# Stick-breaking encoder layer: value matmuls one slot behind their transposes instead of two

## The chip, the cores and the metric

The kernel runs on one core of a Trainium2 chip. The metric is the device time of one execution in microseconds (us). Before the change its median over three runs is 1382.68 us (1381.59 to 1383.48).

The core has five engines that run side by side, each in its own program order, and wait for each other only through semaphores: TensorE (PE in the profile; its weight loads are listed apart as PEld), VectorE (DVE), ScalarE (ACT), GpSimd (POOL) and SyncE (SP), which issues DMAs. TensorE writes to PSUM, which here is eight banks of 128 x 512 float32.

## What is computed

One layer on 1024 tokens of 1024 features, float32: `x += norm(attention(norm(x)))`, then `x += norm(swiglu(norm(x)))`. The attention has 16 heads of 64. Its core, per head, with queries in rows:

```python
z = q @ k.T * scale
before = s < t                        # strictly causal
log_stay = where(before, log_sigmoid(-z), 0)
log_pass = reverse_cumsum(log_stay) - log_stay
a = where(before, exp(log_sigmoid(z) + log_pass), 0)
out = a @ v
```

## The kernel before

Tokens come in reversed order, so that the reverse cumulative sum is a forward scan. Heads are worked on in eight pairs. A pair has four groups: head 0 and 1 with the query rows X = (0, 1, 6, 7) in blocks of 128, then both with Y = (2, 3, 4, 5). Each group has five chunks of its 2304 score columns, so a pair has 20 **slots** and the stage 160, and a short tail of `TAIL_SLOTS` more finishes what is under way. The order of work in a slot is written out by hand, as a software pipeline over all engines. In slot s:

- PE, in this order: the value matmuls (AV, lines 1155 and 1157) of an earlier chunk; one part of the next pair's projections (three matmuls of 512 columns, lines 1083 to 1085); the transposes of a chunk of attention weights into a bank of TB (line 1181), in slots 6 and 9 also those of a piece of V (line 1168); the scores of slot s (lines 1200, 1201); the rest of the projection parts. `PARTS_UPTO` spreads 12 parts over five slots.
- ACT: copies the transposed chunk to `AT_hi`, rounded (line 464), computes two sigmoids of the scores (lines 568, 570), and has in some slots a copy of projected keys or queries, a value copy (line 524) or a weight split (line 456).
- DVE: subtracts `AT_hi` from the transposed chunk into `AT_lo` (line 837, both halves are multiplied with V), then the scans (line 924) and products (line 928) of whole query rows, in some slots the low halves of keys and queries (line 876) and a value addition (line 895).
- POOL: the low half of a split weight unit (line 734, 3 in a pair).

`T_LAG = 7`: the chunk transposed in slot s is the one whose scores were made seven slots before. `AV_LAG = 2`: its AV stand at the head of slot s + 2. There PE waits with `pe.wait_ge(t_lo, ...)` until its `AT_lo` is written. `AT_hi` and `AT_lo` have two buffers, by the parity of the slot. After a group's last AV, ACT copies half of the result (`O_COPY`) and DVE adds the other half (`O_ADD`), at slots fixed in two tables; the pair is counted beside the group, with -1 for the pair before. In the last pair no projections for a further pair are left, only V parts in its first slots. In the tail, PE does the first output projections (`WO_TAIL`, lines 1129 to 1131) between the last AV; they need `o_lo_t` (line 900), which needs `o_hi_t` (line 532) and the additions. The feed-forward part comes behind.

Of the kernel before, what the change touches and what calls it, by code (L numbers as in the profile page):

```python
# [101 lines left out]
def t_blocks(x, c):  # L102

    k, js = T_CHUNKS[x][c]
    out, at = [], 0
    for j in js:
        ks = [m for m in (k, k + 1) if ROWS[x][m] <= j]
        out.append((j, ks, at))
        at += P * len(ks)
    return out, at  # L110
# [17 lines left out]


T_LAG = 7  # L130
AV_LAG = 2
T_PER_STEP = SLOTS + 2
T_START = 2 * NT
V_SLOT = {6: 0, 9: 1}
# [2 lines left out]
def t_slot(s):  # L137

    at = (s - T_LAG) % SLOTS
    n = s + sum(v < s for v in V_SLOT)  # L140
    if s not in V_SLOT:
        return [(n, "a", at)]
    if V_SLOT[s] == 0:
        return [(n, "a", at), (n + 1, "v", 0)]
    return [(n, "v", 1), (n + 1, "a", at)]


def t_index(p, n):

    return T_START - T_LAG + T_PER_STEP * p + n  # L150
# [56 lines left out]

O_COPY = {14: (0, 0), 19: (0, 1), 4: (-1, 2), 9: (-1, 3)}  # L210
O_ADD = {15: (0, 0), 0: (-1, 1), 5: (-1, 2), 10: (-1, 3)}
TAIL_SLOTS = 11
TAIL_O = {0: 0, 1: 1}

WO_TAIL = {1: [(0, 0), (0, 1)], 2: [(0, 2), (1, 0)], 3: [(1, 1), (1, 2)],
# [34 lines left out]
def encoder_layer(nc, x, g_mix_pre, g_mix_post, g_ffn_pre, g_ffn_post, units, out):  # L250
    ctx = ExitStack()
    with ctx:
# [3 lines left out]
        def alloc(stack, name, shape, dt=F32):  # L256
            return stack.enter_context(nc.sbuf_tensor(name, shape, dt))
# [17 lines left out]
        with ExitStack() as one:  # L275
            A = alloc(one, "A", [P, 2, GROUP_W])
            with ExitStack() as qk:
# [10 lines left out]
                AT_hi = alloc(qk, "AT_hi", [P, 2, HALF], F32R)  # L288
                AT_lo = alloc(qk, "AT_lo", [P, 2, HALF], F32R)
# [162 lines left out]
        def _(act):  # L452
# [67 lines left out]
            def o_move(p, group):  # L520

                act.wait_ge(av_done, SLOTS * p + GROUP * (group + 1))
                o_p = acc[:, p, :] if isinstance(p, int) else acc[:, bass.ds(p, 1), :].rearrange("q a n -> q (a n)")
                nc.scalar.activation(values(o_p, group), values_bank(group, OTHER[GROUPS[group][0]]),
                                     ACT.Copy).then_inc(o_moved, 1)
# [8 lines left out]
            def step(p, par, first=False, proj=True, slots=SLOTS):  # L534
                tail = slots < SLOTS
                for s in range(slots):
# [42 lines left out]

                    if s in O_COPY and not (first and O_COPY[s][0] < 0):  # L580
                        dp, group = O_COPY[s]
                        o_move(p + dp, group)
# [15 lines left out]
            def split_at(m, waits):  # L598

                for s, v in waits:  # L600
                    act.wait_ge(s, v)
                split_hi(UNITS1 + m, ring(m), m % 2, 16 * ((UNITS1 + m) // 2 + 1))
# [3 lines left out]
            for t in range(2):  # L606
                act.dma_start(x_in[:, t, :], x_tiles[:, t, :]).then_inc(x_again[t], 16)
            step(PAIRS, 0, proj=False, slots=TAIL_SLOTS)
            split_at(0, [])
# [224 lines left out]
        def _(dve):  # L834
# [46 lines left out]
            def projections(p, par, s, first, proj):  # L881

                if s == 0 and not first:
                    qk_lo(4 * p + 4, "q", par, 1, ACCB[1])
                if proj and s in K_SLOT:
                    qk_lo(4 * p + 4 + K_SLOT[s] + 1, "k", 1 - par, K_SLOT[s], ACCB[K_SLOT[s]])
                if proj and s == Q_SLOT:
                    qk_lo(4 * p + 4 + 3, "q", 1 - par, 0, ACCB[0])

            def o_add(p, group):  # L890

                dve.wait_ge(o_moved, 4 * p + group + 1)
                o_p = acc[:, p, :] if isinstance(p, int) else acc[:, bass.ds(p, 1), :].rearrange("q a n -> q (a n)")
                o = values(o_p, group)
                nc.vector.tensor_tensor(o, values_bank(group, OWN[GROUPS[group][0]]), o, ALU.add).then_inc(o_done, 1)
# [7 lines left out]
            def step(p, par, first=False, proj=True, slots=SLOTS):  # L903
                tail = slots < SLOTS
                for s in range(slots):
# [23 lines left out]
                    if not tail:  # L929
                        projections(p, par, s, first, proj)  # L930
                    if s in O_ADD and not (first and O_ADD[s][0] < 0):
                        dp, group = O_ADD[s]
                        o_add(p + dp, group)
# [7 lines left out]
            step(PAIRS - 1, 1, proj=False)  # L941
            step(PAIRS, 0, proj=False, slots=TAIL_SLOTS)

# [111 lines left out]
        def _(pe):  # L1055
# [79 lines left out]
            def step(p, par, first=False, proj=True, slots=SLOTS):  # L1135
                tail = slots < SLOTS
                for s in range(slots):

                    dp, at = (0, s - AV_LAG) if s >= AV_LAG else (-1, s - AV_LAG + SLOTS)
                    if not (first and s < T_LAG + AV_LAG) and not (tail and s >= T_LAG + AV_LAG):  # L1140
                        z = (at - T_LAG) % SLOTS
                        h, x = GROUPS[z // GROUP]
                        g = next(n for n, kind, _ in t_slot(at) if kind == "a")
                        group = 4 * (p - (s < T_LAG + AV_LAG)) + z // GROUP
                        if z % GROUP == 0 and not (isinstance(group, int) and group < 2):

                            pe.wait_ge(o_done, group - 1)
                        pe.wait_ge(t_lo, t_index(p + dp, g) + 1)
                        blocks_, _ = t_blocks(x, z % GROUP)
                        for m, (j, ks, c0) in enumerate(blocks_):  # L1150
                            w = P * len(ks)
                            dst = OB[h][:, P * ks[0]:P * ks[0] + w]
                            v = V[:, j, 2 * h:2 * h + 2, :].rearrange("p a c -> p (a c)")
                            hi, lo = AT_hi[:, (s - T_LAG) % 2, c0:c0 + w], AT_lo[:, (s - T_LAG) % 2, c0:c0 + w]
                            nc.tensor.matmul(dst, v, hi, start=(z % GROUP == 0 and m == 0), stop=False,  # L1155
                                             skip_group_check=True)
                            mm = nc.tensor.matmul(dst, v, lo, start=False, stop=(z % GROUP == GROUP - 1 and m == 1),  # L1157
                                                  skip_group_check=True)
                        mm.then_inc(av_done, 1)
# [44 lines left out]
                    elif s in WO_TAIL:  # L1204
# [3 lines left out]
                        for t, j in WO_TAIL[s]:  # L1208
                            pe.wait_ge(w_ready, WO_UNIT + j + 1)
                            for c in range(2):  # L1210
                                wo_part(t, c, j)

            step(0, 0, first=True)
            with pe.Fori(0, PAIRS // 2 - 1) as i:
                for u in range(2):
                    step(2 * i + 1 + u, (1 + u) % 2)
            step(PAIRS - 1, 1, proj=False)
            step(PAIRS, 0, proj=False, slots=TAIL_SLOTS)

# [190 lines left out]
```

## Time and profile before

| what | value |
|---|---|
| median of 3 runs | 1382.68 us |
| the profiled execution, its time and its span | 1382.07 us, 1379.6 us |
| PE busy | 1336.1 us (97% of the span) |
| PE weight loads busy | 1115.0 us (81%) |
| DVE busy | 706.0 us (51%) |
| ACT busy | 541.1 us (39%) |
| POOL busy | 360.1 us (26%) |
| mean granted clock of TensorE | 0.99 of full speed |

The profile comes from one execution. The attention stage fills roughly the stretch from 60 to 555 us of the span. Shares of the whole span are means over stages with different limits, so what the change touches is read from stretches of that stage. A row of the timeline gives the start, the duration, the engine, the line of the kernel, the operation, what it writes and reads and its shape, and in brackets the idle time of its engine ahead of it and what ended that. Rows of like instructions that follow each other are merged, with xN. Ends of matmuls are modelled; their starts are the better measure.

### The profile page before, as it was taken

To read this page: it belongs to the slowest core of one execution; us is meant where nothing else is said; L and a number is where in the kernel's file an instruction comes from. 1 tells how busy PE (TensorE), PEld (TensorE's weight loads), DVE (VectorE), ACT (ScalarE), POOL (GpSimd) and SP (SyncE) were. 2 spreads that over 40 slices of the span, in tenths; PEclk is the share of its full clock that TensorE was granted. 3 is DMA by queue.
4 is the path that set the end of the run, shared out by engine and by line. 5 is a ranking of instruction groups with operands and counts; after the bars stand their busy time and mean duration, and the time that the engine had idled before them with its cause. 6 is when DMAs were issued, how large, how long until landed. Compare 5 with 4: busy or idle time off the path is not lost.

```text
span 1379.6 us, 18018 instructions
## 1 busy us (share of the span) xinstructions
PE 1336.1 (97%) x6648; PEld 1115.0 (81%) x6648; DVE 706.0 (51%) x872; ACT 541.1 (39%) x964; POOL 360.1 (26%) x237
## 2 busy tenths in 40 slices
PE   6999999999999977999999999999999999999997
PEld 6888888888888866788888888888888888888885
DVE  7699989889898993335113131322222222223136
ACT  5677767777776773333211212121211111111122
POOL 2111101101110024552542323242323232232343
PEclk9999999999999998999999999999999999999999
DMA  5000000000000013220020201111111111111102
GB/s 213 17 31 32 18 30 31 30 15 31 31 15 31 16 39 130 77 77 16 31 76 16 76 31 61 46 48 43 61 46 46 46 46 46 46 46 46 61 31 107
DMA packets 18340, 66.72 MB, mean 48 GB/s; under 512 B 2032, under 2 KB 2032, under 8 KB 18288
## 3 DMA queue, kind: packets, MB, share of 16 engines
q1 hardware_dynamic: 16704, 60.30, 12.8%
q10 hardware_dynamic: 1584, 5.77, 1.3%
q8 instruction: 28, 0.46, 0.1%
q14 instruction: 24, 0.20, 0.0%
HBM read 61.87 MB, written 4.19 MB: 48 GB/s over the span
## 4 chain that ended last, share of the span: by engine, by line
PE 95%; DVE 4%; ACT 1%; DMA 0%; issue 0%; POOL 0%; SPq 0%; POOLq 0%; ACTq 0%; DVEq 0%
PE bank L1241 12%; PE bank L1239 12%; PE bank L1243 12%; PE bank L1083 6%; PE bank L1085 6%; PE bank L1084 6%; PE bank L1307 5%; PE bank L1306 5%; PE bank L1308 5%; PE bank L1181 4%; PE bank L1155 3%; PE bank L1157 3%; PE bank L1201 2%; PE bank L1200 2%; PE bank L1129 2%; PE bank L1130 2%
## 5 line engine op out<-in xcount | busy, mean ns | idle before, releaser
L734 POOL TENSOR_TENSOR w_lo<-raw,w_hi 128x1024 fp32r<-128x1024 f32 x86 | 209.4, 2440 | 744.2 <-ACT w_hi L456 744.0
L1241 PE MATMUL bank<-hnT_lo,w_hi 128*128 128x512 f32 (+1 forms) x712 | 278.9, 392 | 0.0
L1239 PE MATMUL bank<-hnT_hi,w_hi 128*128 128x512 f32 (+1 forms) x712 | 277.4, 390 | 0.0
L1243 PE MATMUL bank<-hnT_hi,w_lo 128*128 128x512 f32 (+1 forms) x712 | 276.4, 388 | 0.0
L992 DVE TENSOR_TENSOR sg<-bank,sg 128x512 f32<-128x512 f32 x44 | 30.4, 692 | 435.4 <-ACT sg L665 435.4
L456 ACT ACTIVATE w_hi<-raw 128x1024 fp32r<-128x1024 f32 x88 | 92.2, 1059 | 404.2 <-PE bank L1243 353.3
L924 DVE TENSOR_TENSOR_SCAN stay<-stay,diag_one 128x256 f32<-128x256 f32 (+7 forms) x128 | 183.5, 1433 | 3.7 <-ACT stay L570 3.7
L1006 DVE TENSOR_TENSOR y<-bank,y 128x512 f32<-128x512 f32 x160 | 108.8, 690 | 98.7 <-PE bank L1308 81.2
L1239 PEld LDWEIGHTS bank<-hnT_hi,w_hi 128*128 128x128 f32 x712 | 133.7, 188 | 30.6
L1243 PEld LDWEIGHTS bank<-hnT_hi,w_lo 128*128 128x128 f32 x712 | 133.7, 188 | 29.3
L1241 PEld LDWEIGHTS bank<-hnT_lo,w_hi 128*128 128x128 f32 x712 | 133.7, 188 | 28.6
L464 ACT ACTIVATE AT_hi<-bank 128x512 fp32r<-128x512 f32 (+1 forms) x160 | 88.9, 556 | 133.2 <-PE bank L1181 132.5
L1083 PE MATMUL bank<-hnT_hi,w_hi 128*128 128x512 f32 x336 | 133.4, 397 | 0.0
L1085 PE MATMUL bank<-hnT_hi,w_lo 128*128 128x512 f32 x336 | 132.5, 394 | 0.0
L1084 PE MATMUL bank<-hnT_lo,w_hi 128*128 128x512 f32 x336 | 132.2, 394 | 0.0
L837 DVE TENSOR_TENSOR AT_lo<-bank,AT_hi 128x512 fp32r<-128x512 f32 (+1 forms) x160 | 100.6, 629 | 37.2 <-ACT AT_hi L464 36.1
L1307 PE MATMUL bank<-w_lo,h_hi 128*128 128x512 f32 x288 | 114.9, 399 | 0.0
L1306 PE MATMUL bank<-w_hi,h_hi 128*128 128x512 f32 x288 | 113.5, 394 | 0.0
L1308 PE MATMUL bank<-w_hi,h_lo 128*128 128x512 f32 x288 | 112.9, 392 | 0.0
L928 DVE TENSOR_TENSOR A<-A,stay 128x256 f32<-128x256 f32 (+7 forms) x128 | 110.7, 875 | 0.1
L1155 PE MATMUL bank<-AT_hi,V 128*128 128x256 f32 (+1 forms) x320 | 84.1, 286 | 8.8 <-DVE AT_lo L837 8.8
L568 ACT ACTIVATE A<-bank 128x512 f32<-128x512 f32 (+1 forms) x160 | 89.0, 556 | 7.3 <-DVE A L928 4.5
(117 smaller groups left out, 2145.5 us busy)
## 6 DMA issues: line engine op xcount, KB each, us to landing
raw<-in_units SPq DMA_DIRECT2D x98, 512.0 KB, 3.3
acc<-in_x SPq DMA_DIRECT2D x8, 512.0 KB, 9.5
x_in<-in_x ACTq DMA_DIRECT2D x8, 512.0 KB, 3.3
out<-y SPq DMA_DIRECT2D x7, 512.0 KB, 2.6
g_pre_s<-in_mix_pre SPq DMA_DIRECT2D x1, 512.0 KB, 5.2
g_post_t<-in_mix_post ACTq DMA_DIRECT2D x1, 512.0 KB, 7.3
g_ffn_t<-in_ffn_pre ACTq DMA_DIRECT2D x1, 512.0 KB, 3.7
g_out<-in_ffn_post ACTq DMA_DIRECT2D x1, 512.0 KB, 3.9
```

Source lines behind the costliest of these rows:

```text
L734: nc.gpsimd.tensor_tensor(w_lo[slot], raw[:, raw_slot, :], w_hi[slot].bitcast(F32), ALU.subtract).then_inc(w_ready, 1)
L924: nc.vector.tensor_tensor_scan(st, st, diag_one[:, 0:w], 0.0, ALU.mult, ALU.add).then_inc(scan_done, 1)
L1083: nc.tensor.matmul(out_ap, wh, hi, start=(kt == 0), stop=False)
L1084: nc.tensor.matmul(out_ap, wh, lo, start=False, stop=False)
L1085: mm = nc.tensor.matmul(out_ap, wl, hi, start=False, stop=(kt == KT - 1))
L1155: nc.tensor.matmul(dst, v, hi, start=(z % GROUP == 0 and m == 0), stop=False, skip_group_check=True)
L1239: nc.tensor.matmul(dst, wh, hnT_hi[:, kt, cols], start=(kt == 0 and b == 0), stop=False, skip_group_check=halves > 1)
L1241: nc.tensor.matmul(dst, wh, hnT_lo[:, kt, cols], start=False, stop=False, skip_group_check=halves > 1)
L1243: mm = nc.tensor.matmul(dst, wl, hnT_hi[:, kt, cols], start=False, stop=last, skip_group_check=halves > 1)
L1306: nc.tensor.matmul(YB[k % 4][:, :], hh, wh, start=(e == 0), stop=False)
L1307: nc.tensor.matmul(YB[k % 4][:, :], hh, wl, start=False, stop=False)
L1308: mm = nc.tensor.matmul(YB[k % 4][:, :], hl, wh, start=False, stop=(e == 1))
```

## The change

The AV of a chunk move from the head of slot s + 2 to the head of slot s + 1. They read the buffers of the slot before. The value copies on ACT and the additions on DVE move one slot sooner with them, and the tail has one slot less.

```diff
-AV_LAG = 2
+AV_LAG = 1
...
-O_COPY = {14: (0, 0), 19: (0, 1), 4: (-1, 2), 9: (-1, 3)}
-O_ADD = {15: (0, 0), 0: (-1, 1), 5: (-1, 2), 10: (-1, 3)}
-TAIL_SLOTS = 11
+O_COPY = {13: (0, 0), 18: (0, 1), 3: (-1, 2), 8: (-1, 3)}
+O_ADD = {14: (0, 0), 19: (0, 1), 4: (-1, 2), 9: (-1, 3)}
+TAIL_SLOTS = 10
...
-                            hi, lo = AT_hi[:, (s - T_LAG) % 2, c0:c0 + w], AT_lo[:, (s - T_LAG) % 2, c0:c0 + w]
+                            hi, lo = (t[:, (s - AV_LAG - T_LAG) % 2, c0:c0 + w] for t in (AT_hi, AT_lo))
```

## Rows read from the trace of the kernel before

**Rows 1.** The page's chain that ended last, share of the span by engine.
```profile
PE 95%; DVE 4%; ACT 1%; DMA 0%; issue 0%; POOL 0%; SPq 0%; POOLq 0%; ACTq 0%; DVEq 0%
```
**Rows 2.** Windows: stretch, length, busy us per engine, clock, DMA share, GB/s.
```profile
343.21:403.69 60.48, 60.48 (x357) 52.27 (x356) 54.94 (x67) 43.36 (x83) 7.18 (x3) 1.00 0.08 26
...
484.18:516.00 31.82, 23.02 (x144) 20.20 (x142) 31.62 (x37) 24.36 (x48) 6.09 (x2) 0.89 0.12 36
516.00:531.41 15.41, 6.98 (x20) 5.46 (x21) 11.15 (x13) 3.95 (x6) 6.37 (x2) 0.57 0.41 132
```
**Rows 3.** Timeline of slot 8 of a middle pair.
```profile
307.01 0.60 PE L1181 MATMUL bank<-ident,A 128*128 128x128 f32 x4
...
307.65 0.60 ACT L464 ACTIVATE AT_hi<-bank 128x512 fp32r<-128x512 f32 x1 [1.41 <-PE bank L1181]
307.80 0.39 PE L1083 MATMUL bank<-hnT_hi,w_hi 128*128 128x512 f32 x1
...
308.28 0.69 DVE L837 TENSOR_TENSOR AT_lo<-bank,AT_hi 128x512 fp32r<-128x512 f32 x1 [0.81 <-ACT AT_hi L464]
308.50 0.22 PE L1155 MATMUL bank<-AT_hi,V 128*128 128x128 f32 x1
...
308.96 0.39 PE L1083 MATMUL bank<-hnT_hi,w_hi 128*128 128x512 f32 x1
```
**Rows 4.** Timeline where PE does wait for AT_lo, in slot 4.
```profile
352.92 0.55 DVE L837 TENSOR_TENSOR AT_lo<-bank,AT_hi 128x384 fp32r<-128x384 f32 x1
...
353.52 0.33 PE L1155 MATMUL bank<-AT_hi,V 128*128 128x128 f32 x1
...
354.09 0.40 PE L1083 MATMUL bank<-hnT_hi,w_hi 128*128 128x512 f32 x1
```
**Rows 5.** Timeline of DVE in a middle pair.
```profile
347.60 1.39 DVE L876 TENSOR_TENSOR q_lo<-bank,q_hi 64x512 fp32r<-64x512 f32 x2 [0.65 <-ACT q_hi L499]
...
349.63 0.69 DVE L837 TENSOR_TENSOR AT_lo<-bank,AT_hi 128x512 fp32r<-128x512 f32 x1
350.24 2.76 DVE L928 TENSOR_TENSOR A<-A,stay 128x384 f32<-128x384 f32 x1
...
379.72 0.56 DVE L837 TENSOR_TENSOR AT_lo<-bank,AT_hi 128x384 fp32r<-128x384 f32 x1
...
394.53 0.54 DVE L837 TENSOR_TENSOR AT_lo<-bank,AT_hi 128x384 fp32r<-128x384 f32 x1
395.00 0.54 DVE L928 TENSOR_TENSOR A<-A,stay 128x384 f32<-128x384 f32 x1
395.46 0.54 DVE L837 TENSOR_TENSOR AT_lo<-bank,AT_hi 128x384 fp32r<-128x384 f32 x1
...
398.71 1.39 DVE L876 TENSOR_TENSOR q_lo<-bank,q_hi 64x512 fp32r<-64x512 f32 x2 [1.04 <-ACT q_hi L499]
400.13 0.69 DVE L837 TENSOR_TENSOR AT_lo<-bank,AT_hi 128x512 fp32r<-128x512 f32 x1
```
**Rows 6.** Timeline of PE, the first AV at the head of slots 2, 12, 17, 19.
```profile
347.45 0.22 PE L1155 MATMUL bank<-AT_hi,V 128*128 128x128 f32 x1
...
378.23 0.28 PE L1155 MATMUL bank<-AT_hi,V 128*128 128x256 f32 x1
...
393.08 0.28 PE L1155 MATMUL bank<-AT_hi,V 128*128 128x256 f32 x1
...
399.20 0.22 PE L1155 MATMUL bank<-AT_hi,V 128*128 128x128 f32 x1
```
**Rows 7.** Timeline of POOL in the same pair, the first of three.
```profile
350.19 2.39 POOL L734 TENSOR_TENSOR w_lo<-raw,w_hi 128x1024 fp32r<-128x1024 f32 x1 [18.07 <-ACT w_hi L456]
```
**Rows 8.** Timeline of the tail: last additions and the output projections' operands.
```profile
522.97 0.69 DVE L895 TENSOR_TENSOR acc<-bank,acc 64x512 f32<-64x512 f32 x1
...
524.79 1.23 DVE L900 TENSOR_TENSOR o_lo_t<-acc,o_hi_t 128x1024 fp32r<-128x1024 f32 x1 [1.12 <-ACT o_hi_t L532]
...
559.09 0.80 PE L1129 MATMUL bank<-hnT_hi,o_hi_t 128*128 128x512 f32 x1 [2.48 <-DVE o_lo_t L900]
```

## The prediction, made blind

> **What bounds the kernel.** I read the page's chain first: TensorE (PE) carries 95% of what ended last, VectorE (DVE) 4% [rows 1]. A gain or a loss counts here if it makes PE wait less or more. Then I cut the attention stage into head pairs of 20 slots. In a middle pair PE is busy in all of 60.48 us at a granted clock of 1.00, while DVE is busy for 54.94 and ScalarE (ACT) for 43.36 [rows 2]. So nothing that PE needs comes late there, but DVE has only 5.5 us to spare in 60.5. In the last pair, from its seventh slot on, it is the other way round: DVE works 31.62 of 31.82 us, PE 23.02 [rows 2]. The timeline of one slot shows what the change touches. PE transposes a chunk at 307.01, ACT copies it to AT_hi at 307.65, DVE subtracts into AT_lo until 308.97 (308.28 + 0.69), and the next slot's value matmuls (AV) start at 308.50 [rows 3]. Today those belong to the chunk before, whose AT_lo was long done. With the change they need the AT_lo that ends at 308.97.
>
> **The change, part by part.** No instruction is added or removed on any engine: the same AV matmuls, copies, subtractions and DMAs run, so busy sums stay. What moves is the place of a wait. At the head of slot s PE now waits for the subtraction of slot s-1, where one whole slot of about 3 us was between them. PE takes its work in order, so everything behind the wait (projection matmuls, the next transposes, the scores for ACT's sigmoids, and through them DVE's scans) starts later too.
>
> *Price of one wait, queue empty.* In the slot of [rows 3], ACT and DVE had nothing else to do and started 0.04 and 0.03 us after their input. AT_lo still ends 0.47 us after PE is ready (308.97 - 308.50). A PE that really waits adds two small things. From AT_lo's end at 353.47 (352.92 + 0.55) to the AV at 353.52 it is 0.05 us, and from that AV to the next projection matmul (354.09) it is 0.57 us, against 0.46 us (308.50 to 308.96) for the same four matmuls without a wait [rows 3, 4]: 0.11 more. Sum: 0.47 + 0.05 + 0.11 = 0.63 us. The Trainium skill ("TensorE: Matmul & The Clock Gate", Part 2) says that PE pulls weight loads ahead of running matmuls; for one that waits for its operand it can't, which would be up to one 0.19 us load by that rule, where the trace shows 0.11. Elsewhere in the pair sizes differ. For a chunk of 384 columns AT_lo takes 0.55 us for 0.69 [rows 3, 4], and I take the ACT copy as 0.12 shorter in the same proportion. Two score matmuls of 512 columns instead of 384 cover 0.12 us more (0.23 us for 512 columns, a third of the 0.70 from 307.80 to 308.50). That makes 0.63, 0.51, or 0.25 for a short chunk under 512-column scores.
>
> *Which slots pay.* The projection has 12 parts (three matmuls, 0.70 us) in five slots, laid out 2, 2, 3, 2, 3; one goes ahead of the transposes, the rest behind the scores. In slots with two parts behind, the extra 0.70 us covers the 0.63. Twelve slots of twenty have only one. With queues empty they cost 0.25 (slots 0, 5, 11, 16), 0.51 (1, 10, 15) and 0.63 (3, 8, 13, 18), nothing in slot 6, where value transposes follow: 5.1 us per pair. That is the lower bound.
>
> *DVE's queue comes on top.* DVE also runs in order, and a subtraction stands behind the scans and products of the slot before. Today's trace gives the lateness directly: end of AT_lo of slot s minus start of the AV at the head of slot s+1. While DVE has no idle time, PE's waiting doesn't push its work back. So in a stretch of DVE work without idle only the largest lateness counts, and after an idle (DVE waiting for ACT, which follows PE) a new stretch adds its own. A pair has seven such idles of DVE, the first before 347.60, the last before 398.71 [rows 5], five between them in slots 7 to 13. The largest lateness of each stretch [rows 3, 5, 6], with 0.16 (0.05 + 0.11) added:
> slot 1: 350.32 - 347.45 = 2.87, so 3.03;
> slots 7 and 9: not late; slot 8: the slot of [rows 3], 0.47, so 0.63;
> slot 11: 380.28 - 378.23 = 2.05, so 2.21;
> slot 16: 395.07 - 393.08 = 1.99, so 2.15;
> slot 18: 400.82 - 399.20 = 1.62, so 1.78.
> The value additions (0.69 us on DVE [rows 8], today in slots 0, 5, 10 and 15) leave the stretches ahead of slots 1 and 11, since they run one slot sooner: 0.69 less for each. Sum: 2.34 + 0.63 + 1.52 + 2.15 + 1.78 = 8.4 us. Once DVE has caught up, the empty-queue price falls due in slots 3, 5 and 0: 0.63 + 0.25 + 0.25 = 1.1. That gives 8.4 + 1.1, with rounding 9.6 us per pair, 57.6 for the six middle pairs. Upper bound: each of the eleven paying slots is charged the largest lateness of its stretch, 3 x 3.03 + 0.63 + 2 x 2.21 + 3 x 2.15 + 2 x 1.78 = 24.2 us. That needs DVE pushed back by every wait; its idle time grows instead, so I take the 9.6.
>
> *Copies and additions one slot sooner.* They stay two slots and one behind the same matmuls, and cost nothing of their own. At slot 8 ACT's 0.60 us value copy now stands before the weight split, at slot 14 no longer. That shifts GpSimd's 2.4 us subtraction of the weights (like the one at 350.19 [rows 7]) by 0.6 us, once later, once sooner. What it does to DVE is seen at 350.24: a product of 384 columns takes 2.76 us beside it and 0.54 at 395.00 without, while the AT_lo at 349.63, running as it starts, takes its usual 0.69 [rows 5]. So a shift delays products and scans, later at one place and sooner at the other: zero in sum. The Trainium skill ("GPSIMD Engine Reference", Key points) has the two engines share SBUF interfaces where a DVE instruction has two SBUF inputs; by that rule too AT_lo, with one input from PSUM, goes free, and the sum stays.
>
> *First pair.* Chunks begin in slot 7, so slots 0 to 5 are absent: 9.6 - 2.34 - 1.13 = 6.1 us.
>
> *Last pair.* Slots 0 to 5 as before: 2.34 + 1.13 = 3.5. Behind them DVE sets the pace, at 31.82 us over 12 slots, 2.65 each. PE's new loop there (AV 0.57, then 0.64 from the first transpose to AT_hi, 0.63 to AT_lo, 0.69 for it [rows 3, 4], 0.05 to the next AV) is 2.6. Slots heavy on DVE hide it and light ones don't: the subtractions of slots 16 and 17 stand 0.93 us apart (394.53 and 395.46 [rows 5]; the last pair has the same work) and would be 2.3 (the loop less 0.26 for 384 columns). That is 1.4 lost; with one more like it and some smaller ones I take 4 us, between 0 (backlog absorbs it) and 8.
>
> *Tail.* The second group's addition now runs in slot 19, not at 522.97 in the tail's first slot. The o_lo subtraction that the first output projection waits for starts when DVE is free at 523.66 (522.97 + 0.69) instead of 524.79, as its ACT copy is no longer behind the addition [rows 8]: -1.1. The last AVs come a slot sooner, so ACT has the last value copy behind it when the first output projection ends; the 2.48 us wait at 559.09 [rows 8] shortens by about the copy and split in the way, 0.8. Together -1.9.
>
> **Sum:** 57.6 + 6.1 + 3.5 + 4 - 1.9 = 69.3 us. The profiled execution took 1382.07 us (span 1379.6), 0.6 under the median of 1382.68. Forecast 1382.68 + 69.3 = 1452.
>
> **Rivals.**
> *Bare chain only.* The DVE backlog melts as soon as PE waits anywhere, because each wait gives DVE time. For it: DVE is at 91% of a pair and would be at 79% of a 70 us one. Against it: the stretches are made of single 2 us scans in front of a subtraction, and an average doesn't move those. Time: 6 x 5.1 + 3.5 (first, less slots 0 to 5) + 1.6 (last, those slots) - 1.9 = 34, so 1417. Chance 0.14.
> *The clock falls as well.* PE now pauses in each pair, up to 2.3 us at once. For it: in the stretch from 516.00 PE was busy 6.98 of 15.41 us and the clock was at 0.57, near the lower level of 1.2 GHz [rows 2]. Against it: in the 31.82 us before, with pauses of 2 us and less most of the time, it kept 0.89 [rows 2], and a middle pair would still be busy for 60 of 70 us. If it ran at half speed for 7 us of each pair, that is 3.5 us more, 24 in all: 1476. Chance 0.14.
> *Not slower.* PE's wait costs nothing in the middle since copy and subtraction end under the scores and projections, and the tail's 1.9 us remain: 1381. It decides for this if the middle pairs wait under 0.3 us each (1.9 / 6). Slots 7 and 9 speak for it, the rows of the other stretches against. Chance 0.03.
> *More than the sum:* waits that push ACT's sigmoids late enough to make DVE's scans late in turn, beyond 1476: 0.04. The forecast keeps 0.65.
>
> **How the numbers follow.** A measurement of this kernel tells about 0.2%, 2.8 us, from no change. The range must reach toward the bare chain and the clock case: 1424 to 1476 leaves out most of the first and the last tenth. Faster 0.01, same 0.02, slower 0.97, from the same cases.
>
> **What would show it.** Middle pairs of about 70 us, PE busy 60 of them and clock 1.00; a wait of AV (L1155) for AT_lo (L837) as PE's largest, some 11 in a pair, largest at slots 2, 12, 17 and 19; DVE's busy sum unchanged, its idle time up by 9 to 10 us a pair. Pairs near 65.5 us would mean the bare chain; PE busy grown in microseconds with a clock under 1.00, the clock case. The prediction is wrong if PE's wait stays under 2 us in total.

## The result

The changed kernel takes 1456.24 us (median of 4 runs, 1454.91 to 1458.01) against 1382.99 us before: a ratio of 1.0537, 95% interval 1.0523 to 1.0552. Forecast were 1452 us and a range of 1424 to 1476. The profiled execution took 1454.91 us with a span of 1453.1.

The page of the changed kernel: PE's share of the chain falls from the 95% of [rows 1] to 80%, that of DVE grows from 4% to 10%, that of ACT from 1% to 5%.

```profile
span 1453.1 us, 18018 instructions
...
PE 1360.8 (94%) x6648; PEld 1110.9 (76%) x6648; DVE 691.6 (48%) x872; ACT 545.1 (38%) x964; POOL 358.1 (25%) x237
...
PE 80%; DVE 10%; ACT 5%; issue 3%; DMA 0%; DVEq 0%; POOL 0%; ACTq 0%; SPq 0%; POOLq 0%
```

Two of the waits of PE in it, with the total in microseconds, the number of times and the longest. Before, the first was 8.8 us in 6 times, all in the last pair, and the second 9.2 us in 2.

```profile
PE bank L1155 <- DVE AT_lo L837: 65.5, 78, 1.8
...
PE bank L1129 <- DVE o_lo_t L900: 2.6, 2, 1.4
```

The stretches of the changed kernel, as in [rows 2]: first pair from slot 7, six middle pairs, one of them (the sixth of the eight pairs, which answers to the 60.48 us of [rows 2]), last pair to slot 7, from there to the tail, to the first output projection, to the third, the rest.

```profile
61.95:108.85 46.90, 41.69 (x237) 33.65 (x236) 36.16 (x47) 27.73 (x53) 4.76 (x2) 1.00 0.07 23
108.85:532.71 423.86, 379.06 (x2137) 307.56 (x2136) 318.37 (x397) 262.25 (x498) 42.95 (x18) 1.00 0.07 23
391.48:462.13 70.65, 63.19 (x358) 51.33 (x357) 53.08 (x67) 43.70 (x83) 7.17 (x3) 1.00 0.06 23
532.71:556.39 23.68, 21.19 (x120) 16.92 (x119) 16.97 (x22) 14.25 (x28) 0.00 (x0) 1.00 0.00 1
556.39:596.63 40.24, 28.14 (x142) 23.51 (x140) 33.33 (x40) 25.25 (x48) 5.15 (x2) 0.73 0.09 29
596.63:602.30 5.67, 2.92 (x13) 2.15 (x12) 5.61 (x8) 2.96 (x5) 2.86 (x1) 0.50 1.00 338
602.30:632.45 30.15, 29.01 (x138) 23.89 (x139) 7.75 (x11) 12.39 (x19) 15.76 (x7) 0.94 0.37 124
632.45:1453.10 820.65, 809.33 (x3544) 658.06 (x3544) 231.89 (x311) 161.86 (x250) 275.24 (x181) 1.00 0.15 50
```

Their lengths against the same stretches of before, cut at the same PE instructions:

| stretch | before | after | difference | forecast |
|---|---|---|---|---|
| start to the first chunk | 62.26 | 61.95 | -0.3 | 0 |
| first pair from slot 7 | 39.14 | 46.90 | +7.8 | +6.1 |
| six middle pairs | 362.74 | 423.86 | +61.1 | +57.6 |
| last pair to slot 7 | 20.04 | 23.68 | +3.6 | +3.5 |
| last pair from slot 7 | 31.22 | 40.24 | +9.0 | +4 |
| to the first output projection | 10.76 | 5.67 | -5.1 | -1.1 |
| to the third | 32.93 | 30.15 | -2.8 | -0.8 |
| the rest | 820.51 | 820.65 | +0.1 | 0 |
| sum | 1379.6 | 1453.1 | +73.5 | +69.3 |

The loss lies in the attention pairs: 10.2 us in each middle pair, at a granted clock of 1.00. PE's weight loads there are busy for 51.33 us, where it was 52.27. PE "busy" grows from 60.48 to 63.19 us without another instruction. That is how the profile counts: the last matmul ahead of a wait counts for 0.39 us where the next would have started after 0.22, and the first behind it for 0.39 us where the same shape counts for 0.28 without a wait. At some ten waits this makes the 2.7 us, and so the gap that the wait view shows is less than the slot loses. DVE is busy for 53.08 us, 1.9 less than before, and so idle for 17.6 us instead of 5.5.

This is what one of the long waits looks like, the timeline at slot 18 of a middle pair:

```profile
454.32 0.60 PE L1181 MATMUL bank<-ident,A 128*128 128x128 f32 x4
...
454.70 0.60 ACT L499 ACTIVATE q_hi<-bank 64x512 fp32r<-64x512 f32 x1
...
455.32 0.60 ACT L464 ACTIVATE AT_hi<-bank 128x512 fp32r<-128x512 f32 x1
455.33 1.39 DVE L876 TENSOR_TENSOR q_lo<-bank,q_hi 64x512 fp32r<-64x512 f32 x2 [1.18 <-ACT q_hi L499]
...
456.75 0.69 DVE L837 TENSOR_TENSOR AT_lo<-bank,AT_hi 128x512 fp32r<-128x512 f32 x1
...
457.50 0.39 PE L1155 MATMUL bank<-AT_hi,V 128*128 128x256 f32 x1 [1.55 <-DVE AT_lo L837]
```

The transposes end at 454.92. ACT is still copying queries, so AT_hi starts 0.40 us late. DVE had been idle for 1.18 us; then it subtracts the low halves of those queries, and AT_lo starts 0.83 us after AT_hi's end (455.92). It is no scan that PE waits for here.

### The profile page after: what moved, and what is told of

The parts are those of the page before. It is cut to its first block, busy times and chain, and to the rows that moved or that the text cites. A ratio compares the mean times of both kernels' runs of the same rounds, so it can differ in the third digit from the quotient of the medians.

```text
span 1453.1 us, 18018 instructions
## 1 busy us (share of the span) xinstructions
PE 1360.8 (94%) x6648; PEld 1110.9 (76%) x6648; DVE 691.6 (48%) x872; ACT 545.1 (38%) x964; POOL 358.1 (25%) x237
## 4 chain that ended last, share of the span: by engine, by line
PE 80%; DVE 10%; ACT 5%; issue 3%; DMA 0%; DVEq 0%; POOL 0%; ACTq 0%; SPq 0%; POOLq 0%
PE bank L1241 11%; PE bank L1239 11%; PE bank L1243 11%; PE bank L1307 5%; PE bank L1306 5%; PE bank L1308 5%; PE bank L1155 3%; DVE AT_lo L837 3%; PE bank L1083 3%; PE bank L1085 3%; PE bank L1084 3%; PE bank L1181 3%; DVE stay L924 3%; PE bank L1129 2%; PE bank L1130 2%
## 5 line engine op out<-in xcount | busy, mean ns | idle before, releaser
L924 DVE TENSOR_TENSOR_SCAN stay<-stay,diag_one 128x256 f32<-128x256 f32 (+7 forms) x128 | 177.2, 1384 | 3.7 <-ACT stay L570 3.7
L1155 PE MATMUL bank<-AT_hi,V 128*128 128x256 f32 (+1 forms) x320 | 94.7, 318 | 65.9 <-DVE AT_lo L837 65.5
L1155 PEld LDWEIGHTS bank<-AT_hi,V 128*128 128x128 f32 x320 | 61.9, 194 | 110.4 <-DVE AT_lo L837 104.7
L928 DVE TENSOR_TENSOR A<-A,stay 128x256 f32<-128x256 f32 (+7 forms) x128 | 95.4, 756 | 0.1
```

Source lines behind the costliest of these rows:

```text
L924: nc.vector.tensor_tensor_scan(st, st, diag_one[:, 0:w], 0.0, ALU.mult, ALU.add).then_inc(scan_done, 1)
```

## The experiments

Shares of a pair are read as in the table above: from the first transpose of one slot to that of the next, in the fifth of the eight pairs, against the kernel before. The windows shown with the runs are of the sixth or the seventh pair; middle pairs of one kernel differ by under 0.1 us, except where the clock fell. "Head 2" is the start of slot 2, where the value matmuls (AV) wait for the AT_lo of slot 1. Heads left out lose at most 0.1 us in every run. Head 4 can come out below zero, because the kernel before waits 0.17 us there.

| head | forecast | change | old tables | parts behind | half rows | lows later | lows later, half rows |
|---|---|---|---|---|---|---|---|
| 1 | 0.25 | 0.42 | 0.26 | 0.00 | 0.26 | 0.49 | 0.26 |
| 2 | 2.34 | 2.03 | 2.80 | 1.75 | 2.19 | 1.14 | 1.37 |
| 4 | 0.63 | 0.47 | 0.47 | -0.19 | 0.46 | 0.46 | 0.47 |
| 6 | 0.25 | 0.26 | 0.27 | -0.04 | 0.25 | 0.26 | 0.27 |
| 9 | 0.63 | 0.65 | 0.65 | 0.02 | 0.66 | 0.66 | 0.65 |
| 11 | 0 | 0.90 | 0.53 | 0.83 | 0.53 | 0.89 | 0.53 |
| 12 | 1.52 | 0.94 | 1.66 | 0.96 | 0.68 | 0.28 | 0.29 |
| 14 | 0 | 0.65 | 0.64 | 0.02 | 0.65 | 0.65 | 0.65 |
| 16 | 0 | 1.78 | 1.22 | 1.27 | 1.03 | 0.74 | 0.75 |
| 17 | 2.15 | 0.25 | 0.88 | -0.03 | 0.24 | 1.86 | 1.17 |
| 19 | 1.78 | 1.82 | 1.81 | 1.12 | 1.81 | 1.02 | 1.02 |
| 0 | 0 | 0.0 | 0.0 | 0.0 | 0.0 | 0.92 | 0.02 |

**Value matmuls alone: the old tables.** The change without its second part.

```diff
+O_COPY = {14: (0, 0), 19: (0, 1), 4: (-1, 2), 9: (-1, 3)}
+O_ADD = {15: (0, 0), 0: (-1, 1), 5: (-1, 2), 10: (-1, 3)}
+TAIL_SLOTS = 11
```

> Value matmuls one slot behind as in the change, but the value copies and additions stay in their old slots, and the tail keeps its 11 slots. Forecast's theory (a DVE queue ahead of AT_lo, from which the moved additions took 0.69 us at two places of a pair): a middle pair of about 72 us where the changed kernel has 70.65, so 1466 us in all. Rival (the place of the additions doesn't matter, since PE waits in other slots): 70.6 us a pair, 1456 to 1458.

Measured: 1468.76 us, ratio 1.0624 (1.0607 to 1.0640); the window of the sixth pair:

```profile
398.23:469.90 71.67, 63.21 (x357) 51.24 (x356) 55.77 (x67) 43.61 (x83) 7.16 (x3) 1.00 0.07 22
```

The place of the additions counts, as the forecast had it, with 1.0 us a pair instead of 1.4. Heads 2, 12 and 17 get 0.77, 0.72 and 0.63 us worse, which is about one addition each. Heads 1, 11 and 16 get better by 0.16, 0.37 and 0.56: moved to slots 19, 9 and 14, the additions stand in front of other subtractions. The forecast took them out of two places (heads 2 and 12), missed head 17, and didn't put them in anywhere.

**Copies and additions alone.** The kernel before, with the new `O_COPY`, `O_ADD` and `TAIL_SLOTS`, `AV_LAG` still 2.

> The other half alone: value matmuls stay two slots behind, copies and additions one slot sooner, tail of 10 slots. Forecast's theory: the middle pairs stay at 60.45 us, as no wait of PE hangs on the additions; only the first output projection starts about 1.1 us sooner: 1381 to 1382 us. Rival (the tail's gain seen in the changed kernel, some 8 us against the slots before, came from the additions): 1375 to 1378.

Measured: 1379.28 us, ratio 0.9975 (0.9964 to 0.9985), a small gain, between what the theory and its rival gave. The first output projection starts at 525.27 instead of 526.16. Middle pairs did not stay as forecast but are a little shorter (60.31 for 60.45, six times 0.14): the kernel before had a wait of 0.17 us at head 4 [rows 4], and that is gone.

```profile
403.70:464.01 60.31, 60.31 (x357) 52.35 (x356) 54.12 (x67) 43.44 (x83) 7.19 (x3) 1.00 0.08 26
```

**All projection parts behind the scores.** In the changed kernel and, as a control, in the kernel before:

```diff
-    return (parts, []) if first and s == 0 else (parts[:1], parts[1:])
+    return (parts, []) if first and s == 0 else ([], parts)
```

> The changed kernel with all projection parts behind the scores, none ahead of the transposes: 0.70 us more PE work between a chunk's transposes and the value matmuls that need it, the same work in a slot. Forecast's theory (two kinds of wait): the empty-queue waits of 0.25 to 0.65 us go (2.8 us a pair), those at the heads of slots 2, 12, 16 and 19, where DVE's queue ends them, stay nearly whole: 66.5 to 68 us a pair, about 1435 us in all. Rival (all waits are the chain from transposes to AT_lo): each falls by up to 0.70 us, seven to eight of them to nothing, 64 us a pair and 1410. Second rival (DVE alone): no change, 1456.

> Control for the run before: the same order of parts in the kernel before the change. Nothing waits in its middle pairs, so 60.4 us a pair and 1382 to 1384 us by every theory; if scores that come 0.70 us sooner take room from ACT or DVE, it would show here.

Measured: 1423.93 us, ratio 1.0295 (1.0280 to 1.0311), and 1379.26 us, ratio 0.9983 (0.9974 to 0.9992), where the control was expected at 1382 to 1384. The sixth pair, changed kernel first, control second:

```profile
369.05:435.13 66.08, 61.40 (x358) 52.76 (x357) 53.80 (x68) 43.54 (x83) 7.18 (x3) 1.00 0.07 24
```
```profile
342.13:402.24 60.11, 60.11 (x358) 53.26 (x357) 54.98 (x68) 43.38 (x83) 7.21 (x3) 1.00 0.08 27
```

There are two kinds of wait. At heads 1, 4, 6, 9, 14 and 17 the 0.70 us more of cover remove the wait whole, so these were the bare chain from transposes to AT_lo. At heads 2, 11 and 12 nearly all stays, at 16 and 19 the greater part. Here AT_lo is held by what stands ahead of it. All in all 32 us came back of 73, more than the 21 expected for the total. The pair came out just below the range given (66.05 us), and the total went with it: six pairs at 4.6 us and 4.0 in the first make 31.6.

**Half of each scan and product.** Each scan and product runs over the first half of its columns alone; the second half is left out, so these runs are for the time only. Again on both lags:

```diff
+                        w //= 2
                         st, a = stay[:, off:off + w], A[:, h, off:off + w]
```

> The changed kernel with every scan and every product on DVE over the first half of its columns alone: the second half of each row's scan and product is left out. DVE has some 18 us less to do in a pair, so no queue stands ahead of AT_lo. Forecast's theory: only the empty-queue price is left, 5.1 us a middle pair over the run below. Rival (the waits come from the chain and ACT, not from DVE's queue): 10 us a pair as before.

> The kernel before with the same half of the scans and products left out: the base for the run above. PE sets the pace of the middle pairs already, so they stay at 60.45 us; the last pair, which DVE paces, gets some 8 to 12 us shorter: about 1373 us. The difference between the two runs should be 36 to 46 us by the forecast's theory (5.1 a pair, more in the last pair, where PE has nothing to cover the chain), 73 by the rival.

Measured: 1449.42 us, ratio 1.0483 (1.0467 to 1.0499), and 1371.12 us, ratio 0.9922 (0.9907 to 0.9938). They are 78 us apart, where I expected 36 to 46 and the rival 73: a clear miss. DVE has 13.7 us less to do in a pair (I had said 18) and PE waits nearly as before. Two pairs of the first, one of the second:

```profile
388.01:458.89 70.88, 64.86 (x357) 52.45 (x356) 39.42 (x67) 43.71 (x83) 7.14 (x3) 0.98 0.07 23
458.89:528.16 69.27, 63.25 (x358) 51.28 (x356) 39.43 (x67) 43.68 (x83) 7.17 (x3) 1.00 0.07 23
```
```profile
403.23:463.47 60.24, 60.24 (x358) 52.24 (x357) 41.30 (x66) 43.39 (x83) 7.18 (x3) 1.00 0.08 27
```

So 9.0 us a pair stay (69.27 - 60.24) of 10.2. Of the waits, those at heads 11, 12 and 16 get shorter, by 1.4 us together; those at heads 2 and 19 don't. The timeline of slot 18 shows why: DVE sits idle for 1.97 us and PE still waits.

```profile
381.23 0.60 ACT L464 ACTIVATE AT_hi<-bank 128x512 fp32r<-128x512 f32 x1
381.24 1.39 DVE L876 TENSOR_TENSOR q_lo<-bank,q_hi 64x512 fp32r<-64x512 f32 x2 [1.97 <-ACT q_hi L499]
...
382.66 0.69 DVE L837 TENSOR_TENSOR AT_lo<-bank,AT_hi 128x512 fp32r<-128x512 f32 x1
...
383.41 0.39 PE L1156 MATMUL bank<-AT_hi,V 128*128 128x256 f32 x1 [1.54 <-DVE AT_lo L837]
```

My theory that DVE's scans are what makes AT_lo late falls here, for the two longest waits. The new one: the query copies, four on ACT (0.6 us each) ahead of AT_hi and then two subtractions on DVE (1.39 us together) ahead of AT_lo. Half of the pairs took 1.6 us more; in them the clock fell behind the wait at head 2 (last section).

**Low halves one slot later.** The new theory's own test, in the changed kernel:

```diff
-                if s == 0 and not first:
+                if s == 1 and not first:
...
-                if proj and s in K_SLOT:
+                if proj and s - 1 in K_SLOT:
...
-                if proj and s == Q_SLOT:
+                if proj and s - 1 == Q_SLOT:
```

> The changed kernel with DVE's low halves of keys and queries (1.39 us) taken one slot later, behind that slot's AT_lo instead of ahead of it. New theory, formed after half the scans and products were left out and 9 of the 10.2 us a pair stayed (the long waits at the heads of slots 2 and 19 come from the query copies, on ACT ahead of AT_hi and on DVE ahead of AT_lo, not from scans): AT_lo there starts 0.83 us sooner, both waits shrink by that, 69.0 us a middle pair and 1443 to 1446 us. Rival (ACT's four copies alone set those waits): 70.6 a pair, 1455.

Measured: 1450.60 us, ratio 1.0485 (1.0469 to 1.0501), 69.86 us a middle pair: a gain, but less than the 69.0 and 1443 to 1446 expected. Heads 2 and 19 shrink by 0.89 and 0.80 us, as the 0.83 said, and heads 12 and 16 by 0.66 and 1.04, for the key copies do the same there. That is 3.4 us. But 2.6 come back, 1.61 of them at head 17 and 0.92 at head 0. DVE ahead of head 17 shows the new place:

```profile
374.16 0.66 DVE L929 TENSOR_TENSOR A<-A,stay 128x512 f32<-128x512 f32 x1
374.85 0.69 DVE L876 TENSOR_TENSOR k_a<-bank,k_a 64x512 fp32r<-64x512 f32 x1
375.55 0.69 DVE L876 TENSOR_TENSOR k_b<-bank,k_b 64x512 fp32r<-64x512 f32 x1
376.27 0.56 DVE L837 TENSOR_TENSOR AT_lo<-bank,AT_hi 128x384 fp32r<-128x384 f32 x1
```

AT_hi was there at 374.65 (374.16 + 0.49); AT_lo starts 1.62 us later, behind a scan, a product and the two low halves that all belong to the slot before.

**Both together.** Low halves later, and again the second half of each scan and product left out:

> The same with every scan and product over the first half of its columns alone, the second half left out. New theory: with both queues gone only the empty-queue price (5.1 to 5.3 us over 60.24) and ACT's late AT_hi (0.9 and 0.4 us in slots 1 and 18) are left, so 66.8 to 67.6 us a middle pair, and as the wait at slot 2 gets under 1.5 us the clock no longer falls there in every other pair: 1428 to 1433 us. Rival (scans matter once the low halves are out of the way): 69 us a pair as without the move.

Measured: 1431.62 us, ratio 1.0359 (1.0343 to 1.0375), 67.90 us a pair, just above the 66.8 to 67.6 expected:

```profile
446.25:514.15 67.90, 63.21 (x357) 51.25 (x356) 40.24 (x67) 43.72 (x83) 7.19 (x3) 1.00 0.07 23
```

That is 2.8 us a pair less than the change, where the one remedy gave 0.8 and the other 1.4 (70.65 to 69.27). Here the scans do matter: the 0.92 at head 0 are gone again, and 0.69 of the 1.61 at head 17. And in no middle pair does the clock fall. Over the base of 60.24 us 7.7 are left; by the forecast's prices 5.1 of them are the empty-queue price. Head 19 keeps 1.02 us, which is that price of 0.63 and the 0.40 by which AT_hi was late at slot 18.

**Low halves later and parts behind.**

> The changed kernel with both remedies: low halves one slot later and all projection parts behind the scores. If they act on different waits: 66.05 less 1.0 to 1.6, so 64.4 to 65.0 us a pair and 1410 to 1416 us in all. Rival (the cover of 0.70 us already took what the low halves cost): 66.0 and 1423.

Measured: 1420.32 us, ratio 1.0268 (1.0252 to 1.0284), 65.53 us a pair for 66.05. That is only 0.5 of the 1.0 to 1.6 us expected. Head 17 now waits 1.85 us and head 0 0.94: the gain is given back at the same two heads as without the cover. Total and pair both miss the expectation.

**The change in the last pair and the tail alone.** PE takes its AV with a lag from a small function; at the switch it does both chunks:

```diff
+                    for lag in av_lags(s, first, proj, tail):
+                        dp, at = (0, s - lag) if s >= lag else (-1, s - lag + SLOTS)
...
+    if last:
+        return (2, 1) if s == 0 else (1,)
+    if tail:
+        return (1,)
+    return (2,)
```

> The change made only in the last pair and the tail; the first seven pairs are as before. If the stretches of the changed kernel's trace add up (last pair 3.6 + 9.0 longer, from there to the end of the first output projections 7.9 shorter), 1387 to 1388 us. Forecast's own numbers for these stretches give 1388 (3.5 + 4 - 1.9 = 5.6). Rival (the clock at its lower level in the last pair comes from the waits in the pairs before): no low clock there, 1380 to 1383.

Measured: 1390.20 us, ratio 1.0060 (1.0047 to 1.0074). The pairs before the switch keep their time of 60.45 us, the stretch with the switch has 1.3 us more, and from the last pair's slot 7 the clock is at 0.80 though the seven pairs before are unchanged:

```profile
403.63:465.39 61.76, 61.18 (x362) 52.80 (x360) 56.23 (x68) 43.38 (x83) 7.17 (x3) 1.00 0.08 26
491.25:531.08 39.83, 26.07 (x142) 21.61 (x141) 33.27 (x40) 24.98 (x48) 5.21 (x3) 0.80 0.10 34
```

The low clock doesn't need the waits of the pairs before. It is 8 us over the kernel before instead of the 5 expected. The switch itself is a wait that the changed kernel doesn't have, and the last pair's slots 0 to 6 take 25.86 us for 23.68 there.

**The change in the tail alone,** from the tail's slot 2, with the new tables in the last pair and the tail:

```diff
+    if tail:
+        return (2, 1) if s == 2 else (1,) if s > 2 else (2,)
```

> The change only where it has cover: value matmuls two slots behind up to the tail's slot 1, in slot 2 those of both chunks, one slot behind from there; copies and additions one slot sooner in the last pair and the tail, tail of 10 slots. No pair pays a wait. Theory (the end of the stage gains from an earlier last addition, and from earlier operands of the first and the third output projection): 1.1 to 3 us, 1380 to 1382 us. Rival (that time is hidden anyway): 1383.

Measured: 1379.70 us, ratio 0.9981 (0.9972 to 0.9990). Between the first and the third output projection it takes 30.47 us for 32.93; that covers the gain.

**The small gains together.** New tables throughout, parts behind, one slot behind from the tail's slot 2:

> The three small gains on the old lag together: value matmuls two slots behind, copies and additions one slot sooner throughout, all projection parts behind the scores, and one slot behind only in the tail from its slot 2. They shorten different stretches (middle pairs 60.45 to about 60.1; from the last pair's end to the output projections), so most should add: 1375 to 1378 us. Rival (each only took the same 2.8 us of slack): 1379.

Measured: 1378.71 us, ratio 0.9973 (0.9961 to 0.9984). The fastest version that leaves nothing out, and no faster than the tables alone as far as the intervals tell. It is also short of the 1375 to 1378 expected. Middle pairs take 60.11 us, to the third projection it is 556.22 for 559.09. The gains don't add: that fits the rival (1379) more than my sum.

## Why the prediction came out right

The sum was 69.3 us and the span grew by 73.5 (the median by 73.3). The direction, the two kinds of cost and the place of the loss were right. That the size came so close is in part luck: in the middle pairs the forecast is off by 0.6 us in sum (9.6 for 10.2), but by 6.6 us if the errors of the single heads are added without their signs. By its steps:

1. *Price of one wait, queue empty.* Held. Forecast 0.63, 0.51, 0.25 us; heads 9 and 14 lose 0.65, heads 6 and 17 lose 0.26 and 0.25, and in the run with half rows head 11 loses 0.53. At head 4 it is 0.47, and the kernel before had 0.17 there already. No run shows a pair that pays these prices and nothing else.
2. *Which slots pay.* Held: the heads behind slots with two parts lose nothing. Run "parts behind" shows the cause.
3. *DVE's queue on top.* The size held (forecast 8.4 + 1.1, measured 10.2 with the empty prices), the content only in part. Heads 2 and 19, the lateness of the slots 1 and 18, came out at 2.03 and 1.82 for 2.34 and 1.78. But the text laid it to "single 2 us scans in front of a subtraction". Half the scans and products took away only 1.4 us. What stands at heads 2 and 19 is the query copies, on ACT and on DVE. For head 19 the rows of slot 18 are in the section on the result, for head 2 these are the ones of slot 1:

```profile
394.57 0.60 PE L1181 MATMUL bank<-ident,A 128*128 128x128 f32 x4
...
395.87 0.60 ACT L464 ACTIVATE AT_hi<-bank 128x512 fp32r<-128x512 f32 x1
...
397.29 0.69 DVE L837 TENSOR_TENSOR AT_lo<-bank,AT_hi 128x512 fp32r<-128x512 f32 x1
```

AT_hi starts 0.70 us after the transposes' end and AT_lo 0.82 us after AT_hi's. The two delays add to 1.5 us here and to 1.2 us at slot 18; less the usual 0.07 and with the empty price of 0.51 and 0.63 they are all of the two waits. The share on DVE is shown by the run with the low halves later; the share on ACT is read from the rows, and no run moved ACT's copies. The rule "only the largest lateness of a stretch counts" misplaced one: it had 2.15 us at head 17 and nothing at 14 and 16, and measured are 0.25, 0.65 and 1.78. A wait at one head lets DVE catch up, so a stretch breaks; further heads then pay at least the empty price. Head 17 was also relieved of an addition (0.63 us by the old tables).
4. *Copies and additions one slot sooner.* The additions gave 1.0 us a pair, forecast 1.4, since they land in front of other subtractions (old tables). GpSimd's subtraction was to shift "zero in sum". It didn't: in the kernel before it ran beside a product (2.76 us [rows 5]) and a scan (1.84 us), and in the changed kernel it hardly meets either. The first row is of before, the rest are of the changed kernel.

```profile
391.58 1.84 DVE L924 TENSOR_TENSOR_SCAN stay<-stay,diag_one 128x384 f32<-128x384 f32 x1
...
446.56 0.95 DVE L924 TENSOR_TENSOR_SCAN stay<-stay,diag_one 128x384 f32<-128x384 f32 x1
...
397.90 0.55 DVE L928 TENSOR_TENSOR A<-A,stay 128x384 f32<-128x384 f32 x1
...
398.46 2.39 POOL L734 TENSOR_TENSOR w_lo<-raw,w_hi 128x1024 fp32r<-128x1024 f32 x1 [22.39 <-ACT w_hi L456]
```

The two take 1.50 us instead of 4.60. So the sign "DVE's busy sum unchanged" failed: it fell by 1.9 us a pair, and DVE's idle time grew by 12.0 us, not 9 to 10. What this took from the waits no run separates.
5. *First pair.* 7.8 for 6.1 us: the same terms as in 3.
6. *Last pair and tail.* The term of 4 us and that of -1.9 were both mis-sized, and that their errors cancel is luck: +3.6, +9.0, -5.1, -2.8 make 4.7, forecast 5.6. From slot 7 to the first output projection it is 3.9 us, forecast 2.9. The text counted 12 slots of 2.65 us in DVE's pace there; slots 7 to 19 are 13, so it is 2.40 us a slot (31.22 / 13), and a PE loop of 2.6 is not hidden behind that. In the kernel before DVE was some 4 us behind PE when the tail began (AT_lo of its first slot started 4.4 us after AT_hi was there), and PE waited 6.8 us ahead of the projection. The changed kernel pays along the way and waits 1.4 us there. Part of the 9.0 is the clock. The first row is of the kernel before; the others are of "parts behind", "low halves later and parts behind" and "low halves later", which have the program of the changed kernel in this stretch, as "last pair" has (39.83 us at 0.80):

```profile
484.18:515.40 31.22, 22.53 (x141) 19.95 (x140) 31.02 (x37) 23.76 (x48) 6.09 (x2) 0.89 0.11 35
...
523.58:565.67 42.09, 30.75 (x142) 25.97 (x140) 32.58 (x39) 25.31 (x47) 4.99 (x2) 0.67 0.09 30
...
521.77:562.65 40.88, 27.42 (x142) 23.09 (x141) 32.84 (x39) 25.08 (x47) 5.21 (x3) 0.76 0.11 35
...
552.11:592.35 40.24, 25.82 (x141) 21.69 (x140) 33.74 (x40) 25.01 (x48) 5.15 (x2) 0.82 0.09 29
```

At a clock of 0.67 the stretch takes 42.09 us, at 0.80 and 0.82 39.83 and 40.24, and the changed kernel's 40.24 at 0.73 and the 40.88 at 0.76 lie between or near: some 2 us for 0.14 of the clock. From 0.73 to the 0.89 of before it is about the same step, so an estimate is that some 2 of the 9.0 us are the clock and 7 are waits.
7. *The rivals.* The bare chain alone (1417) was about half of the truth: 34 of 73 us. The clock case doesn't hold in the middle pairs of the changed kernel, at 1.00; in its last pair the clock is lower than before (0.73 for 0.89), and it also falls in the middle pairs in the run with half rows, and once in that with the old tables (0.50 around 117 to 120 us). "Not slower" and "more than the sum" are excluded by the 61 us lost in the middle pairs and by the total. Of the four heads named as the largest waits, 2 and 19 are, 12 is fourth with 0.94 us behind head 16, and 17 is not one of them.

## What to carry to other kernels

A pipeline's lag is paid at every place where the chain copy, subtraction, use is longer than the producer's own work in between. Measure that chain on a slot with idle engines (here 0.63 us), then add what stands ahead of each link in its engine's order, one by one. An engine with 9% of idle time over a pair can still be late at every slot that holds a lump of copies; look at which instruction stands in front before giving it a name, and expect a lump that is moved to be late again one slot on.

## What the runs showed of the hardware

PE's clock fell behind pauses that are shorter than the ones I had looked at before. In the run with half rows, at slot 2 of every other pair, PE waits for 1.86 us, the row of the timeline that comes first, and then the windows go on without another pause:

```profile
394.57 0.39 PE L1156 MATMUL bank<-AT_hi,V 128*128 128x256 f32 x1 [1.86 <-DVE AT_lo L837]
```
```profile
393.00:395.00 2.00, 0.42 (x3) 0.43 (x4) 1.74 (x4) 1.91 (x3) 0.01 (x1) 1.00 0.00 0
395.00:397.00 2.00, 2.00 (x10) 1.65 (x9) 0.00 (x0) 0.00 (x1) 2.00 (x1) 0.63 0.00 0
397.00:399.00 2.00, 2.00 (x6) 1.52 (x6) 1.48 (x2) 1.57 (x3) 0.36 (x1) 0.52 0.29 72
399.00:401.00 2.00, 2.00 (x14) 1.68 (x13) 0.21 (x1) 0.00 (x0) 0.00 (x0) 1.00 0.50 195
```

The clock goes to its lower level of 1.2 GHz (0.63 and 0.52 of full speed in two windows) and is back at 399; the pair takes 70.88 us for 69.27. The pairs between them have the same wait (1.86 to 1.91 us in all six) and keep the clock, so the length of the wait alone doesn't decide. In the last pair of the changed kernel the clock stays at 1.00 through 18.5 us in which PE is busy for only 10.81, and is at the lower level in the stretch behind it. What PE did before the clock fell is the second row below; the busy time of the slow stretch says nothing of the cause.

```profile
575.00:605.70 30.70, 23.55 (x85) 19.40 (x85) 24.93 (x27) 17.12 (x28) 10.20 (x4) 0.50 0.31 103
556.39:574.90 18.51, 10.81 (x76) 8.88 (x74) 15.96 (x22) 12.13 (x26) 0.00 (x0) 1.00 0.00 1
```

At half speed the same matmuls count as busy for longer, so the 23.55 us there are less work than they read. In the kernel before the clock falls in the last pair too, for less of the time (0.89 from slot 7 on).
